# Attention ahead of the mLSTM work in each step, on TensorE and VectorE

## The reference

```
z = x @ w_in                      # split into q,k,v of attention, an indexer, q,k,v,o and gates of the mLSTM
y_a = sparse attention            # 8 heads of 64; each query keeps its 128 best keys by the indexer's score
q_m, k_m = silu(causal depthwise conv over 4 tokens (q_m, k_m))
y_m = mLSTM                       # 4 heads of 128: weights = (q k^T) * decay, num = weights @ v, then a norm per head
x = LN(alpha*x + [y_a, y_m] @ w_out)
x = LN(alpha*x + MoE(x))          # 32 experts in 4 groups, 2 experts per token
x = x + sigmoid(x @ w_g) * (p @ w_p)
```

## Time and profile before

| | |
|---|---|
| median of three executions | 667.53 us |
| profiled execution | 667.36 us |
| its span, first to last instruction | 665.6 us |
| mean granted TensorE clock | 0.984 |
| TensorE busy | 628.4 us (94%) |
| VectorE busy | 367.2 us (55%) |
| steps 12 to 31 in the trace | about 104 to 264 us |

### The profile page before, as it was taken

The page is one execution under the profiler, slowest core; times in us unless marked ns, Lnnn a source line. Parts: engine busy times, 40 slices in busy tenths (PEclk is TensorE's granted clock), DMA queues, the critical chain, the costliest instruction groups (busy, mean ns, idle before and its releaser), DMA issues.

```text
span 665.6 us, 10286 instructions
## 1 busy us (share of the span) xinstructions
PE 628.4 (94%) x3869; PEld 442.8 (67%) x3869; DVE 367.2 (55%) x850; ACT 178.3 (27%) x345; POOL 162.9 (24%) x173
## 2 busy tenths in 40 slices
PE   8999998999989978999789998999999999969997
PEld 6868978878868867887555555555555555525885
DVE  7779998688677685768561122211221122128946
ACT  4673324343252242402111111111111111143221
POOL 2518372001010010421032322333233323110100
PEclk9999999999999998999899998999999999998999
DMA  7503241013003100199948999999999999958003
GB/s 245 218 33 110 113 152 70 1 62 130 1 0 149 42 1 30 47 352 401 388 174 322 397 417 416 417 415 412 416 416 413 412 415 415 407 232 319 0 1 126
DMA packets 30503, 151.22 MB, mean 227 GB/s; under 512 B 7372, under 2 KB 7628, under 8 KB 16496
## 3 DMA queue, kind: packets, MB, share of 16 engines
q1 hardware_dynamic: 24048, 142.08, 53.8%
q0 software_dynamic: 6400, 8.42, 3.5%
HBM read 148.36 MB, written 14.68 MB: 245 GB/s over the span
## 4 chain that ended last, share of the span: by engine, by line
PE 69%; DVE 9%; issue 4%; ACT 1%; POOL 1%; DMA 1%; ACTq 0%; DVEq 0%; POOLq 0%
PE bank L2098 21%; PE bank L2113 12%; PE bank L1739 7%; PE bank L1741 7%; PE bank L1740 7%; PE bank L2088 3%; PE bank L1883 2%; PE bank L2105 2%; PE bank L2011 2%; PE bank L1834 1%; PE bank L1892 1%; PE bank L1862 1%; PE bank L1849 1%; DVE res L1239 1%; DVE res L1213 1%
## 5 line engine op out<-in xcount | busy, mean ns | idle before, releaser
L1651 DVE COPY rows_x<-bank 128x128 f32<-128x128 f32 x40 | 11.6, 291 | 187.7 <-issue 120.5
L1739 PE MATMUL bank<-w_hi,a_hi 128*128 128x384 f32 (+1 forms) x240 | 88.1, 367 | 0.0
L1741 PE MATMUL bank<-w_hi,a_lo 128*128 128x384 f32 (+1 forms) x240 | 86.6, 361 | 0.0
L1740 PE MATMUL bank<-w_lo,a_hi 128*128 128x384 f32 (+1 forms) x240 | 86.5, 360 | 0.0
L743 POOL DMA_INDIRECT pair_dram<-rows_x,row_put x40 | 40.5, 1013 | 160.0 <-ACT rows_x L1005 156.0
L2098 PE MATMUL bank<-raw,rows_x 128*64 128x256 f32 x640 | 72.8, 379 | 1.4 <-DVE rows_x L1625 0.8
L1739 PE MATMUL bank<-a_hi,w_hi 128*128 128x512 f32 (+1 forms) x176 | 69.6, 395 | 2.8 <-DVE a_lo L1421 1.5
L1741 PE MATMUL bank<-a_hi,w_lo 128*128 128x512 f32 (+1 forms) x176 | 67.6, 384 | 0.0
L1740 PE MATMUL bank<-a_lo,w_hi 128*128 128x512 f32 (+1 forms) x176 | 67.6, 384 | 0.0
L2098 PEld LDWEIGHTS bank<-raw,rows_x 128*64 128x64 f32 x640 | 46.1, 137 | 32.2 <-issue 11.5
L737 POOL DMA_INDIRECT y<-x_dram,row_got x40 | 41.2, 1029 | 36.0 <-DVE row_put L1586 23.4
(11 more groups left out here) (269 smaller groups left out, 1020.4 us busy)
## 6 DMA issues: line engine op xcount, KB each, us to landing
raw<-in_w_exp_dram SPq DMA_DIRECT2D x48, 1024.0 KB
slots<-in_w_exp_dram SPq DMA_DIRECT2D x27, 1024.0 KB
rows_x<-in_w_exp_dram SPq DMA_DIRECT2D x14, 1024.0 KB
raw<-in_w_in_dram SPq DMA_DIRECT2D x19, 512.0 KB, 3.4
y<-in_w_exp_dram SPq DMA_DIRECT2D x7, 1024.0 KB
raw<-in_w_wide_dram SPq DMA_DIRECT2D x4, 1536.0 KB, 7.8
raw<-in_w_out_dram SPq DMA_DIRECT2D x4, 1024.0 KB, 7.0
raw<-pair_dram SPq DMA_DIRECT2D x8, 512.0 KB, 6.4
```

Of the source, the lines that this page charges most:

```text
L1739: t_.matmul(o, lh, rh, start=first, stop=False)
L1740: t_.matmul(o, lh, rl, start=False, stop=False)
L1741: return t_.matmul(o, ll, rh, start=False, stop=last)
```

## The change

In VectorE's `work` the block with `convolve_end` and `lstm_weight` moves from the front of the step to behind the attention, the split of a weight piece and `normalise`. The wide split, the variance, the decay and the convolution of other heads stay behind it. In TensorE's `work` the two `lstm_qk` calls of a step move from ahead of the attention to behind it; `lstm_num` and `lstm_broadcast` stay in front. No instruction is added or removed, and ScalarE, GpSimd and SyncE keep their order.

```diff
@@ VectorE, work(g, j)
                 now = STEPS * g + j
-                for h in range(HM):
-                    if CONV_END[h] == now:
-                        convolve_end(h, 0)
-                        convolve_end(h, 1)
-                    if 0 <= now - HEAD_QK[h] < 2:
-                        lstm_weight(h, 2 * (now - HEAD_QK[h]))
-                        lstm_weight(h, 2 * (now - HEAD_QK[h]) + 1)
                 for h in range(NG):
                     if 0 <= now - ATTEND[h] < 6:
                         attention(h, now - ATTEND[h])
...
                 for h in range(NG):
                     if 0 <= now - ATTEND[h] <= 3:
                         normalise(h, now - ATTEND[h])
+                for h in range(HM):
+                    if CONV_END[h] == now:
+                        convolve_end(h, 0)
+                        convolve_end(h, 1)
+                    if 0 <= now - HEAD_QK[h] < 2:
+                        lstm_weight(h, 2 * (now - HEAD_QK[h]))
+                        lstm_weight(h, 2 * (now - HEAD_QK[h]) + 1)
                 if POOL_WIDE <= g < NG and j == 0:
                     split_wide(g)
@@ TensorE, work(g, j)
                     if BROADCAST[h] == now:
                         lstm_broadcast(h)
+                for h in range(NG):
+                    if 0 <= now - ATTEND[h] < 6:
+                        attention(h, now - ATTEND[h])
+                for h in range(HM):
                     if 0 <= now - HEAD_QK[h] < 2:
                         lstm_qk(h, 2 * (now - HEAD_QK[h]))
                         lstm_qk(h, 2 * (now - HEAD_QK[h]) + 1)
-                for h in range(NG):
-                    if 0 <= now - ATTEND[h] < 6:
-                        attention(h, now - ATTEND[h])
```

## The result

The changed kernel takes 678.17 us (median of four executions, 675.58 to 683.98) where the kernel before takes 667.85 on the same chip: a ratio of 1.0162, 95% interval 1.0124 to 1.0200, or +10.3 us where +7.5 was forecast. Measured again later beside the experiments, the ratio was 1.0137 (1.0105 to 1.0168), or +8.7 us. The profiled span went from 665.6 to 675.8 us.

A forecast was written before the change was run, and what follows sets the result against it. TensorE, busy 94% of the span, was taken as the bound, with every shift carried to the end. The terms 4.8 + 4.4 − 1.1 − 0.6 = +7.5 us gave 675.0 us, range 669.5 to 679.5.

The forecast's parts named there:

- The mechanism: In the steps, TensorE's attention runs ahead of its wait; VectorE's convolve_end goes behind normalise, which waits for the step's exponentials.
- Step 21: TensorE's 0.70 us wait for a late copy can go as VectorE gets ahead: −0.6 us, between 0 and −0.7.
- Step 24: Product starts at 202.65 against 196.87, behind exponentials that follow ScalarE's rounding: +4.4 us, bounds +2.9 and +5.9.
- Step 14: TensorE idles 5 us for convolve_end: +3.25 us and one clock fall of 1.54, +4.8 us, bounds +3.25 and +6.3.
- Step 30: No normalise here; product 1.85 us later but attention already done: −1.1 us, the middle of −1.9 and −0.4.
- Step 31: Weights come up to 4 us later, but lstm_num stands behind a whole project: counted as nothing.
- Clock up: Rival: clock stays up in all three waiting steps, as attention runs shortly before each wait; +3.5, 671.0 us, chance 0.15.
- Low for longer: Rival: idleness of 5 and some 7 us costs a second low clock stretch each; +10.6, 678.1 us, chance 0.08.
- Absorbed: Rival: slack before the transfer-set expert stage takes up the shift, or waits lie elsewhere; 667.5 us, chance 0.10.
- Filled waits: Rival: attention fills TensorE's waits and convolve_end comes in time behind it; −8.6, 658.9 us, chance 0.05.

The follow-up runs named there:

- the waits filled: Changed kernel with spare products of 128x512 put into TensorE's waits in steps 14, 24 and 30, results unused: 673.49 us, ratio 1.0055.
- Head 0 alone: Kernel before with the changed order for head 0 only (steps 14 and 15), heads 1 to 3 as before: 671.89 us, ratio 1.0040.
- the two experiments on it: Changed kernel with head 3's last products ahead of attention on TensorE, 680.91 us; with second steps' products and weights in front on both engines, 681.06 us.
- TensorE's half: Kernel before with only TensorE's reordering, for heads 0 to 2; VectorE and head 3 as before: 665.81 us, ratio 0.9954.
- The best kernel: Against the kernel before: convolve_end in front, first steps' products and weights behind attention, outputs of heads 1 and 2 one step later: 658.14 us, ratio 0.9845.

## Why the prediction was right

**The mechanism** held in each of its links. TensorE's attention ran ahead of the wait and `convolve_end` behind `normalise`. The forecast had the product of step 14 at 120.8 (120.56 came, in steps that begin 0.17 us earlier) and the distance from the end of `project` to the product of step 24 at 8.5 us (8.11, 207.37 − 199.26). With `convolve_end` alone put back, the loss became a gain; with the waits filled, steps 14 and 24 kept +3.05 and +2.44, where the forecast had +3.25 and +2.9 for a clock that stays up.

**Step 21** was right: −0.6 forecast, −0.56 measured. **Step 24** came out at 4.4 against 4.49, and that is in part luck: with the clock up it was +2.44 and not +2.9, and the low clock cost 2.05 and not 1.54. The two errors cancel.

**Step 14**, forecast as +4.8, measured +5.8. The wait was right; the term mis-sized was the fall of the clock, counted as 1.54 us. It cost 2.76, since the clock stayed low into `project`. Head 0 alone, with the same wait, cost 4.62. Six profiles of this wait lie between 4.62 and 6.05, inside the bounds of 3.25 and 6.3 and mostly nearer the upper one.

**Step 30**, forecast as −1.1, the middle between −0.4 and −1.9, measured −0.14. The short gaps brought the clock down, and early: the second group of transposes took 0.87 us instead of the 0.52 it took in the kernel before, and the next `project` ran half a microsecond longer. This was the sentence that read a rule out of the earlier trace rows, that 1.95 us of idleness leaves the clock up and 2.70 does not; the 1.99 us that brought it down shows that three waits were too few for such a rule. With the clock up the step brought 2.16 us, somewhat more than the 1.9 worked out.

**Step 31**, forecast as nothing, cost 1.0 us. I looked for late weights in front of `lstm_num` and found a whole `project` between. In step 31 there is none: `lstm_num` of head 3 follows directly, and the pv products wait 0.80 us for ScalarE's copy of the last v piece, a time in which the old order ran the two products. This is the one loss that the forecast did not have; the two experiments on it show that TensorE's old order alone does not get it back and that both engines' does; VectorE's alone was not run.

**The sum**: about 1.0 us each in steps 14, 30 and 31 are the 3 us between +7.5 and the +10.6 of the table (its steps begin 0.17 us earlier, which makes the +10.4 behind them). Sorted by cause, the waits and the filled attention of steps 14, 24 and 30 were put at 3.25 + 2.9 − 1.9 = 4.25 us and came to 3.05 + 2.44 − 2.16 = 3.33; the clock was put at 3.85 and came to 6.83; step 31 was put at nothing and came to 1.0. So the mechanism was right, and the size of the low clock's term was the main error. The Trainium skill, "TensorE: Matmul & The Clock Gate", section "What's actually happening", says that for modelling the ramp penalty is under 1% of a typical kernel span, and not to fit to a specific cold count. Leaving it out would have given +6.7, further off: here the 6.8 us are 1.0% of the span, but two thirds of the change's effect.

**The rivals.** Clock up: no, it fell in all three steps. Low for longer: true of step 14, while in step 24 the low clock cost 2.05 us and not twice 1.54; that its total, 678.1, is the one measured is chance, since the rest came from steps 30 and 31. Absorbed: no, +10.4 at 284 us and +10.3 at the end. Filled waits: true of TensorE's half, and with `convolve_end` left in front the order was faster than before by 3.9 us, not by the 8.6 worked out.

## What to carry to other kernels

When work is moved ahead of a wait on one engine, look at what the other engine moved behind: here two instructions, 1.3 us together, that end the wait were put behind the round trip mask, exponential, normalise. In the steps with a long wait, the order that won is the one in which the producer of the long wait goes first on its engine and the consumer last on its own. The best kernel also took other work, an output, out from in front of that producer. Where the last step of a pipeline has no filler behind it, count it by itself.

## What the hardware showed that I had not expected

The same wait cost differently in different profiles. 1.95 us of idleness left the clock at 2.4 GHz in the first profile and 1.99 us brought it to 1.2 GHz in another, 1.66 us more for the step. After the same wait of 4.74 us the low stretch ended at about 124 in one profile and 126 in another, 1.2 us apart in cost; why is not shown. From these numbers, a forecast for this kernel should carry the clock as a spread for each wait, from nothing or 1.5 us to nearly three, not as a fixed price.
